# Diagonal products of a PEER layer as 64x64 tiles of the PE array

## The chip, the cores and the metric

The kernel runs as one program on one core of a Trainium2 chip. The metric is device time in microseconds (us) from start to end of the program. Before the change it is 4265.8 us, the median of three runs (4264.91 to 4271.66).

## The reference, cut to what matters

One layer of a diffusion backbone is applied to 128 context tokens and 1024 latent tokens of width 1024, all in float32. A token mixer comes first (two recurrences and a gated merge), then PEER: for every token, 8 heads choose 16 experts each out of 16384, and each chosen expert is one row `u` and one row `v` of a table.

```
def block(args):                      # hb: tokens x 1024, eb, gb: tokens x 8 heads x 16
    act = gelu(einsum('td,thkd->thk', hb, u_tab[eb]))
    return einsum('thk,thkd->td', gb * act, v_tab[eb])
...
out   = PEER(rmsnorm(x) * (1 + sc2) + sh2)
y     = rmsnorm(x + g2 * out, norm_f)
```

So a token has 128 chosen experts, and its output is the sum over them of `coefficient * v row`. Every row is gathered by an index that depends on the data. `u` and `v` of one expert lie side by side in memory (2048 floats, 8 KB).

## The kernel before, in words

The program has two parts. The first (to about 1275 us of the trace) is the mixer and its merge; the change touches it nowhere. The second is PEER. It handles the 1152 tokens as 9 tiles of 128 tokens, one token per partition. A tile has 128 chosen experts per token, one "slot" each: 4 pairs of heads x 32 slots. The slots are processed in rounds of 8 (`RING = 8`), because there are 8 ring buffers `RG[:, s, :]` of 128 x 2048 floats (1 MB).

One slot passes through five engines:

- **GpSimd queue** (`stage_b_pool`, `fetch`): waits until `v_used` says that the last user of this ring buffer is done (line 414), then issues one indirect DMA (line 415) that gathers 128 rows of 8 KB, one per partition.
- **VectorE** (`stage_b_dve`, `rounds`): when the rows have landed, a multiply with sum (line 845) gives the dot product with `u`. After every second slot (`GRP = 2`) `coef` (line 835) multiplies GELU by gate.
- **ScalarE** (`stage_b_act`, `rounds`): GELU (line 630), then for each slot a diagonal matrix (line 636): the identity times the slot's coefficient per partition, 128 x 128, into `DG[:, s, :]`, and counts `diag_r` up.
- **TensorE** (`stage_b_pe`, `rounds`): multiplies that diagonal matrix by the `v` half of the ring buffer, in two products of 512 columns (line 541), which accumulate in PSUM banks 0 and 1. All 128 slots of a tile accumulate there. Then it counts `v_used` up, which lets GpSimd refill the buffer.

The order of each engine's work is written out by hand. Between slots, at positions given by dictionaries called `between`, TensorE also does the queries, transposes and scores of the next tile (lines 482, 490, 498, 504), in banks 2 to 6; ScalarE copies them out, and VectorE searches the best keys. While tile 0 runs, this next-tile work is packed more tightly (`two_pairs_between`).

At the end of a tile VectorE copies the expert numbers and the next tile's input to where they are used (`next_tile`, lines 864 to 866), and the loop over tiles goes round. VectorE then does slots 0 and 1 of the new tile, and after slot 1 `read_sum` (line 877): it waits for all `v_used` of the old tile, reads banks 0 and 1, multiplies by the gate row `G2B` into `Y`, and counts `acc_free` up. TensorE waits for that, clears the two banks with products of a zero matrix (`clear`, line 550; two products), and only then goes on with the diagonal products of the new tile. After slot 5 `residual` (lines 883, 884) adds the residual and sums squares; after slot 11 `norm` makes the output. There are 8 such tile changes: from tile 0 into the loop over tiles 1 to 7, six from turn to turn of that loop, and one out of it to tile 8. After the last tile `read_sum`, `residual` and `norm` stand at the very end.

## Time and profile before

| what | value |
|---|---|
| median of three runs | 4265.8 us |
| the profiled execution's own time | 4269.28 us |
| its span, from first to last instruction | 4267.2 us |
| PE busy | 3688.6 us (86%) |
| VectorE busy | 2605.5 us (61%) |
| ScalarE busy | 1080.1 us (25%) |
| GpSimd busy | 1307.4 us (31%) |
| mean granted TensorE clock | 0.971 of full speed |

"Busy" is the time in which an engine has at least one instruction under way. PE's matmuls and PE's weight loads (PEld) are listed apart and overlap. Times of single instructions come from this one profiled execution. The granted clock is 1.0 at 2.4 GHz and 0.5 at 1.2 GHz; a figure between is a mean over a stretch.

### The profile page before, as it was taken

Reading aid. Unit: us, or ns where it says so; the run is one execution under the profiler, and the core shown is the slowest. Engines: PE = TensorE matmul, PEld = TensorE weight load, DVE = VectorE, ACT = ScalarE, POOL = GpSimd, SP = SyncE. Lnnn points to the kernel's source line nnn. Section 1 sums busy time; section 2 is a strip of 40 time slices with the busy share of each in tenths; the row PEclk is TensorE's granted clock in tenths of the full one; section 3 lists DMA queues with packets and bytes.
Section 4 is the critical chain, followed back from the end, with each engine's and each line's share of the span. In section 5 each row is a group of like instructions: output and inputs, shape, how many; then the busy total and the mean of one; then the engine's idle time right before and its main releaser. Section 6 shows DMA issues by size and latency. Waiting matters only on the chain.

```text
span 4267.2 us, 40396 instructions
## 1 busy us (share of the span) xinstructions
PE 3688.6 (86%) x10642; PEld 1802.4 (42%) x10642; DVE 2605.5 (61%) x6424; ACT 1080.1 (25%) x2672; POOL 1307.4 (31%) x1174
## 2 busy tenths in 40 slices
PE   8999999999997888888898888888888888888776
PEld 3766767555443333333333333333333333333222
DVE  4545455333238677667767766766776677677555
ACT  2534534000002223222222222222222222222211
POOL 0000000000003434444444444444444444444432
PEclk9999999999998999999999999999999999999999
DMA  4010000311429999999999999999999999999998
GB/s 175 16 35 20 25 10 32 129 69 69 182 73 361 420 400 407 420 420 401 413 419 400 420 422 399 421 419 393 421 421 389 420 422 400 417 417 420 413 422 356
DMA packets 187700, 1310.84 MB, mean 307 GB/s; under 512 B 24082, under 2 KB 25618, under 8 KB 36274
## 3 DMA queue, kind: packets, MB, share of 16 engines
q0 software_dynamic: 165888, 1208.03, 68.6%
q1 hardware_dynamic: 21684, 101.33, 6.2%
q8 instruction: 52, 0.85, 0.1%
q14 instruction: 76, 0.62, 0.1%
HBM read 1299.28 MB, written 10.00 MB: 307 GB/s over the span
## 4 chain that ended last, share of the span: by engine, by line
PE 47%; DMA 32%; DVE 9%; issue 9%; ACT 3%; DVEq 0%; POOL 0%; POOLq 0%; SPq 0%; ACTq 0%
DMA arena<-in_uv,arena 32%; PE ps L541 16%; PE ps L1101 9%; PE ps L449 9%; DVE arena L845 3%; PE ps L490 3%; PE ps L473 3%; PE ps L1145 2%; PE ps L1095 2%; ACT arena L636 1%; PE ps L1162 1%; PE ps L1117 1%; DVE arena L791 1%; PE ps L504 0%; DVE arena L795 0%
## 5 line engine op out<-in xcount | busy, mean ns | idle before, releaser
L541 PE MATMUL ps<-arena 128*128 128x512 f32 x4608 | 2201.6, 619 | 471.0 <-ACT arena L636 469.3
L845 DVE CUSTOM_DVE_ANT_0 arena<-arena 128x1024 f32<-128x1024 f32 x1152 | 1409.5, 1226 | 892.5 <-DMA arena<-in_uv,arena 831.4
L415 POOL DMA_INDIRECT arena<-in_uv,arena x1152 | 1301.2, 1130 | 1688.5 <-PE ps L541 1536.2
L541 PEld LDWEIGHTS ps<-arena 128*128 128x128 f32 x4608 | 864.1, 196 | 1723.1 <-issue 885.0
L636 ACT ACTIVATE arena<-ident,arena 128x128 f32<-128x128 f32 x1152 | 398.6, 393 | 1063.1 <-DVE arena L835 1063.1
L1101 PE MATMUL ps<-arena 128*128 128x384 f32 x1152 | 387.8, 493 | 15.9 <-issue 14.0
L406 POOL IOTA arena<- 128x16 f32 x1 | 0.1, 147 | 1244.6 <-DMA x_scratch<-arena 1244.6
L449 PE MATMUL ps<-arena 128*128 128x384 f32 x1152 | 373.9, 487 | 2.2 <-DMA arena<-in_w_mg 2.0
L630 ACT ACTIVATE arena<-arena 128x2 f32<-128x2 f32 x576 | 117.1, 203 | 1001.5 <-DVE arena L845 1001.4
L1101 PEld LDWEIGHTS ps<-arena 128*128 128x128 f32 x1152 | 217.8, 193 | 160.6 <-issue 22.8
L449 PEld LDWEIGHTS ps<-arena 128*128 128x128 f32 x1152 | 218.1, 190 | 159.7 <-issue 6.0
L490 PE MATMUL ps<-arena 128*128 (+1 forms) x576 | 284.1, 592 | 1.3 <-ACT arena L596 1.3
L1486 DVE SCALAR_TENSOR_TENSOR arena<-arena,dec,ps 128x128 f32<-128x128 f32 x272 | 94.6, 348 | 125.4 <-PE ps L1145 118.0
L490 PEld LDWEIGHTS ps<-arena 128*128 128x128 f32 x576 | 109.3, 190 | 138.7 <-issue 138.7
L697 DVE TENSOR_TENSOR arena<-ps,arena 128x384 f32<-128x384 f32 x48 | 24.5, 552 | 231.2 <-ACT arena L583 231.2
L473 PE MATMUL ps<-arena 128*128 128x512 f32 x288 | 123.8, 592 | 1.6 <-DVE arena L701 1.6
L583 ACT ACTIVATE arena<-ps 128x384 f32<-128x384 f32 x48 | 20.9, 488 | 362.4 <-PE ps L449 362.4
L1210 ACT ACTIVATE arena<-ps 128x384 f32<-128x384 f32 (+2 forms) x88 | 45.1, 517 | 245.9 <-PE ps L1101 201.5
L1264 ACT ACTIVATE arena<-ps 32x128 f32<-32x128 f32 x288 | 77.3, 268 | 85.9 <-PE ps L1135 82.8
L835 DVE TENSOR_TENSOR arena<-arena 128x2 f32<-128x2 f32 x576 | 90.3, 157 | 8.9 <-ACT arena L630 8.9
L845 DVE DVE_READ_ACCUMULATOR2_ANT arena<- 128x1 f32 x1152 | 94.5, 82 | 0.0
L1145 PEld LDWEIGHTS ps<-arena 128*128 128x128 f32 x576 | 74.9, 192 | 23.6 <-ACT arena L1264 11.5
(200 smaller groups left out, 2438.8 us busy)
## 6 DMA issues: line engine op xcount, KB each, us to landing
arena<-in_w_mod SPq DMA_DIRECT2D x12, 2048.0 KB, 23.3
arena<-in_uv,arena POOLq DMA_INDIRECT x1152, 10.3
arena<-in_w_in SPq DMA_DIRECT2D x28, 512.0 KB, 3.4
arena<-in_w_mg SPq DMA_DIRECT2D x8, 1536.0 KB, 6.2
arena<-x_scratch SPq DMA_DIRECT2D x18, 512.0 KB, 11.7
arena<-in_w_q SPq DMA_DIRECT2D x4, 2048.0 KB, 20.2
arena<-in_xT SPq DMA_DIRECT2D x4, 1152.0 KB, 13.4
arena<-in_x_tok SPq DMA_DIRECT2D x9, 512.0 KB, 4.7
```

The costliest lines, as they stand in the source:

```text
L415: nc.gpsimd.indirect_dma_start(out=RG[:, s, :], out_offset=None, in_=uv, in_offset=bass.IndirectOffsetOnAxis(ap=IDXS[:, par_, s:s + 1], ax ...
L449: mm = nc.tensor.matmul(PS[:, b + g, 0:CH], WMG[u][:, w0 + k, :], src[:, k, sl], start=(k == 0), stop=(k == nk - 1))
L473: mm = nc.tensor.matmul(PS[:, 2 * (t % 2) + n, :], MG[:, k, t * P:(t + 1) * P], WO[:, k, n * 512:(n + 1) * 512], start=(k == 0), stop=(k = ...
L490: mm = nc.tensor.matmul(PS[:, 4, :], H2T[:, k, :], WQ[:, k, bass.ds(i * 512, 512)], start=(k == 0), stop=(k == KD - 1))
L541: mm = nc.tensor.matmul(PS[:, n, :], DG[:, s, :], RG[:, s, D + n * 512:D + (n + 1) * 512], start=False, stop=False, skip_group_check=True)
L630: A(GEL[:, sl], PRE[:, sl], ACT.Gelu_apprx_tanh).then_inc(gel_r, 1)
L636: A(DG[:, s, :], ident[:], ACT.Copy, scale=COEF[:, s:s + 1]).then_inc(diag_r, 1)
L835: v.tensor_tensor(COEF[:, sl], GEL[:, sl], GATE[:, bass.ds(i * RPP * RING + q * RING + g * GRP, GRP)], ALU.mult).then_inc(coef_r, 1)
L845: ins = v.tensor_tensor_reduce(RG[:, s, 0:D], RG[:, s, 0:D], H2C, 1.0, 0.0, ALU.mult, ALU.add, PRE[:, s:s + 1])
L1101: mm = nc.tensor.matmul(z, w[:, k, :], hT[:, k, n * CH:(n + 1) * CH], start=(k == 0), stop=(k == KD - 1))
L1145: mm = nc.tensor.matmul(PS[:, 5 + it % 2, j * P:(j + 1) * P], KET[:, it % 2, j, :], Vt[:, tile_of(it), :], start=True, stop=True)
L1486: ins = v.scalar_tensor_tensor(out=to, in0=st, scalar=dec[:, d, c:c + 1], in1=PS[:, 5 + it % 2, j * P:(j + 1) * P], op0=ALU.mult, op1=ALU.add)
```

## The change: what it does

For each pair of slots TensorE waits once, for both diagonals. A diagonal matrix has nothing outside its two diagonal 64 x 64 blocks. So each slot's diagonal is now stored as 128 x 64: rows 0 to 63 hold the first block, rows 64 to 127 the second (`halves` is the identity in that form, made once by ScalarE into the tile `ones`, which is no longer used by then). Each product of 128 x 128 by 512 columns becomes two products of 64 x 64 by 512 columns, one per half of the partitions. The even slot of a pair writes them straight, and the odd slot swapped: rows 0 to 63 go to output partitions 64 to 127 and the other way round. So the four products of a pair with the same columns use four different quarters of the array. The two halves of the rows have accumulators of their own, banks 0 and 1 for rows 0 to 63, banks 2 and 3 for rows 64 to 127, and in each of them one half of the partitions holds the straight sum and the other the swapped sum.

What follows from that: `clear` zeroes four banks; the transposes of the input of the next tile (`front`) move from banks 2 and 3 to banks 4 and 7; `read_sum` copies the swapped halves into `Y` and adds the straight halves (four instructions on 64 partitions each, with a wait after each copy), and the multiplication by `G2B` moves to `residual`.

```
 def rounds(t, i, between):                         # TensorE
     for q in range(RPP):
-        for s in range(RING):
-            n0 = (t * ROUNDS + i * RPP + q) * RING + s + 1
-            pe.wait_ge(diag_r, n0)
+        for g in range(RING // GRP):
+            n0 = (t * ROUNDS + i * RPP + q) * RING + (g + 1) * GRP
+            wait_alone(pe, diag_r, n0)
             for n in range(2):
-                mm = nc.tensor.matmul(PS[:, n, :], DG[:, s, :], RG[:, s, D + n * 512:D + (n + 1) * 512],
-                                      start=False, stop=False, skip_group_check=True)
-            mm.then_inc(v_used, 1)
-            at = q * RING + s
-            if at in between:
-                between[at]()
+                for turned in range(GRP):
+                    s = g * GRP + turned
+                    for r in range(2):
+                        rows = slice(r * HALF, (r + 1) * HALF)
+                        c = (r + turned) % 2
+                        mm = nc.tensor.matmul(PS[c * HALF:(c + 1) * HALF, 2 * r + n, :], DG[rows, s, :],
+                                              RG[rows, s, D + n * 512:D + (n + 1) * 512],
+                                              start=False, stop=False, skip_group_check=True)
+            mm.then_inc(v_used, GRP)
+            for at in range(q * RING + g * GRP, q * RING + (g + 1) * GRP):
+                if at in between:
+                    between[at]()
 def clear():
-    for n in range(2):
+    for n in range(4):
         nc.tensor.matmul(PS[:, n, :], zero[:], zero[:, 0:1].to_broadcast([P, 512]), ...)
 def front(tn):
-    mm = nc.tensor.transpose(PS[:, 2 + k // 4, ...], H2N[...], ident[:])
+    mm = nc.tensor.transpose(PS[:, 4 + 3 * (k // 4), ...], H2N[...], ident[:])
 def stage_b_act(act):                              # ScalarE
+    for r in range(2):
+        rows = slice(r * HALF, (r + 1) * HALF)
+        A(halves[rows], ident[rows, rows], ACT.Copy).then_inc(hv_r, 1)
...
-    A(DG[:, s, :], ident[:], ACT.Copy, scale=COEF[:, s:s + 1]).then_inc(diag_r, 1)
+    A(DG[:, s, :], halves, ACT.Copy, scale=COEF[:, s:s + 1]).then_inc(diag_r, 1)
 def read_sum(self):                                # VectorE
     dve.wait_ge(v_used, (t + 1) * ROUNDS * RING)
-    v.tensor_tensor(Y, PS[:, 0:2, :]..., G2B, ALU.mult).then_inc(acc_free, 1)
+    halves_of = [slice(r * HALF, (r + 1) * HALF) for r in range(2)]
+    acc = [PS[:, 2 * r:2 * r + 2, :]... for r in range(2)]
+    for r in range(2):
+        self.ch(v.tensor_copy(Y[halves_of[r]], acc[r][halves_of[1 - r]]))
+    for r in range(2):
+        ins = v.tensor_tensor(Y[halves_of[r]], acc[r][halves_of[r]], Y[halves_of[r]], ALU.add)
+    ins.then_inc(acc_free, 1)
 def residual(self):
+    self.ch(v.tensor_tensor(Y, Y, G2B, ALU.mult))
     self.ch(v.tensor_tensor(Y, Y, XE, ALU.add))
```

## Rows read from the trace of the kernel before

**Rows 1.** The page: busy time of PE, transfer rate in 40 slices, the gather's queue.
```profile
PE 3688.6 (86%) x10642; PEld 1802.4 (42%) x10642; DVE 2605.5 (61%) x6424; ACT 1080.1 (25%) x2672; POOL 1307.4 (31%) x1174
GB/s 175 16 35 20 25 10 32 129 69 69 182 73 361 420 400 407 420 420 401 413 419 400 420 422 399 421 419 393 421 421 389 420 422 400 417 417 420 413 422 356
q0 software_dynamic: 165888, 1208.03, 68.6%
```
**Rows 2.** Stretches: busy time and count per engine, PEclk, DMA share, GB/s.
```profile
2240.00:2260.00 20.00, 17.34 (x42) 7.44 (x41) 15.87 (x56) 4.19 (x13) 10.26 (x9) 0.91 1.01 422
2300.00:2320.00 20.00, 19.55 (x52) 8.64 (x51) 14.07 (x28) 7.42 (x17) 9.78 (x9) 1.00 0.80 313
...
4220.00:4240.00 20.00, 14.92 (x33) 5.75 (x32) 10.29 (x21) 3.59 (x12) 7.62 (x9) 1.00 1.01 421
```
**Rows 3.** The same in stretches of 10 us, start of the gathering and end of tile 0.
```profile
1290.00:1300.00 10.00, 1.81 (x2) 0.84 (x3) 9.79 (x23) 1.91 (x5) 0.00 (x0) 0.50 1.02 428
1310.00:1320.00 10.00, 10.00 (x27) 4.53 (x26) 2.68 (x8) 1.27 (x4) 2.80 (x3) 1.00 0.94 350
...
1580.00:1590.00 10.00, 10.00 (x25) 4.39 (x24) 9.54 (x35) 2.17 (x7) 3.10 (x4) 1.00 0.98 361
```
**Rows 4.** The page's groups of instructions: diagonal products, queries.
```profile
L541 PE MATMUL ps<-arena 128*128 128x512 f32 x4608 | 2201.6, 619 | 471.0 <-ACT arena L636 469.3
L490 PE MATMUL ps<-arena 128*128 (+1 forms) x576 | 284.1, 592 | 1.3 <-ACT arena L596 1.3
```
**Rows 5.** Timeline, weight loads and a run of matmuls of line 541 (start, duration).
```profile
2400.42 1.88 PE L541 MATMUL ps<-arena 128*128 128x512 f32 x4
2400.43 0.19 PEld L541 LDWEIGHTS ps<-arena 128*128 128x128 f32 x1 [0.24 <-issue]
...
2400.85 0.19 PEld L541 LDWEIGHTS ps<-arena 128*128 128x128 f32 x1 [0.24 <-issue]
...
2401.28 0.19 PEld L541 LDWEIGHTS ps<-arena 128*128 128x128 f32 x1 [0.24 <-issue]
```
**Rows 6.** Waits from 1500 to 4260 us: who for whom, us, times, longest.
```profile
PE ps L550 <- DVE arena L877: 42.1, 8, 7.0
```
**Rows 7.** Timeline of one tile change inside the tile loop.
```profile
2610.64 7.28 PE L541 MATMUL ps<-arena 128*128 128x512 f32 x16 [1.73 <-ACT arena L636]
...
2620.84 1.23 DVE L845 CUSTOM_DVE_ANT_0 arena<-arena 128x1024 f32<-128x1024 f32 x1 [5.79 <-issue]
...
2623.13 1.22 DVE L877 TENSOR_TENSOR arena<-ps,arena 128x1024 f32<-128x1024 f32 x1
...
2624.41 3.49 PE L550 MATMUL ps<-zero 128*128 128x512 f32 x4 [6.49 <-DVE arena L877]
...
2627.73 7.25 PE L541 MATMUL ps<-arena 128*128 128x512 f32 x16
...
2630.39 1.14 POOL L415 DMA_INDIRECT arena<-in_uv,arena  x1 [10.76 <-PE ps L541]
```
**Rows 8.** Timeline of another such tile change, clear and first products.
```profile
3283.52 3.78 PE L550 MATMUL ps<-zero 128*128 128x512 f32 x4 [6.51 <-DVE arena L877]
3287.10 10.03 PE L541 MATMUL ps<-arena 128*128 128x512 f32 x20
3291.03 1.95 POOL L415 DMA_INDIRECT arena<-in_uv,arena  x1 [12.31 <-PE ps L541]
```
**Rows 9.** VectorE's groups by form: copies and two-input operations.
```profile
L866 DVE COPY arena<-arena 128x1024 f32<-128x1024 f32 x8 | 5.6, 698 | 0.0
L1465 DVE COPY arena<-ps 128x128 f32<-128x128 f32 x36 | 10.2, 283 | 0.0
L1467 DVE TENSOR_TENSOR arena<-ps,arena 128x128 f32<-128x128 f32 x36 | 10.2, 284 | 11.9 <-PE ps L1162 11.9
```
**Rows 10.** Timeline of the last tile change.
```profile
3936.51 0.94 POOL L415 DMA_INDIRECT arena<-in_uv,arena  x1 [0.30 <-issue]
...
3936.96 1.99 PE L550 MATMUL ps<-zero 128*128 128x512 f32 x4 [1.31 <-DVE arena L877]
...
3941.04 1.22 DVE L845 CUSTOM_DVE_ANT_0 arena<-arena 128x1024 f32<-128x1024 f32 x1 [1.26 <-DMA arena<-in_uv,arena]
```
**Rows 11.** Timeline of the program's end.
```profile
4251.39 7.13 PE L541 MATMUL ps<-arena 128*128 128x512 f32 x16 [1.27 <-ACT arena L636]
...
4258.56 1.22 DVE L877 TENSOR_TENSOR arena<-ps,arena 128x1024 f32<-128x1024 f32 x1 [4.85 <-PE ps L541]
4259.82 1.23 DVE L883 TENSOR_TENSOR arena<-arena 128x1024 f32<-128x1024 f32 x1
```

More of the change, by code:

```diff
@@ L56 @@
 GRP = 2
+HALF = P // 2
 P_LB, P_CW, P_CB, P_BR, P_BI, P_LAM, P_HN, P_H0, NPAR = 0, 4, 8, 9, 11, 13, 15, 16, 18
@@ L274, in build @@
     QS, QTS = QQ[:, 0:512], QQ[:, 512:1024]
-    DG = DG_.rearrange("p (s c) -> p s c", s=RING)
+    DG = DG_[:, 0:RING * HALF].rearrange("p (s c) -> p s c", s=RING)
     SCS, SCW = SC_[:, 0:512], SC_[:, 512:1024]
@@ L299, in build @@
     PRE, GEL, COEF = sm(RING), sm(RING), sm(RING)
+    halves = ones[:, 0:HALF]
     PHL = sb("places", [P, 2, 2, TOPK], U32)[:]
@@ L314, in build @@
     acc_free, e_sq, e_sd, y_r, y_st = (sem(x) for x in ("acc_free", "end_square", "end_sd", "y_ready", "y_stored"))
-    it_r = sem("iota_ready")
-    PAIR_STEPS, FRONT_STEPS, END_STEPS = 16, 2, 2
+    it_r, hv_r = sem("iota_ready"), sem("half_identities_ready")
+    PAIR_STEPS, FRONT_STEPS, END_STEPS = 16, 2, 5
     def row(ap):
@@ L481, in front @@
             for k in range(KD):
-                mm = nc.tensor.transpose(PS[:, 2 + k // 4, (k % 4) * P:(k % 4 + 1) * P],
+                mm = nc.tensor.transpose(PS[:, 4 + 3 * (k // 4), (k % 4) * P:(k % 4 + 1) * P],
                                          H2N[:, k * P:(k + 1) * P], ident[:])
@@ L595, in rows_out @@
             for n in range(2):
-                cp = A(H2T_[:, n * 512:(n + 1) * 512], PS[:, 2 + n, :], ACT.Copy)
+                cp = A(H2T_[:, n * 512:(n + 1) * 512], PS[:, 4 + 3 * n, :], ACT.Copy)
             cp.then_inc(h2t_e, 1)
@@ L652, in stage_b_act @@
         rows_out(0)
+        act.wait_ge(hv_r, 2)
         for i in range(2):
@@ L876, in read_sum @@
                 dve.wait_ge(v_used, (t + 1) * ROUNDS * RING)
-                v.tensor_tensor(Y, PS[:, 0:2, :].rearrange("p b c -> p (b c)"), G2B, ALU.mult).then_inc(acc_free, 1)
+                halves_of = [slice(r * HALF, (r + 1) * HALF) for r in range(2)]
+                acc = [PS[:, 2 * r:2 * r + 2, :].rearrange("p b c -> p (b c)") for r in range(2)]
+                for r in range(2):
[3 more added lines that the diff above has]
+                ins.then_inc(acc_free, 1)
             def residual(self):
```

## The prediction

> **What bounds the kernel now.** I read the page first, then stretches of equal length, then the timeline at the places where the stretches differ. The page invites a wrong reading: PE is busy 86% of the span [rows 1], and its costliest group is the one that is changed, 2201.6 us [rows 4]. But the transfer rate in the same page stands at 420 to 422 GB/s in most slices from the fourteenth on and falls only in every third or so. The stretches say what that is: in the middle of a tile the DMA share is 1.01 at 422 GB/s, while PE is busy 17.34 of 20 us; in the last tile, where PE has nothing but diagonal products, PE is busy only 14.92 of 20 and the rate is the same, 421 [rows 2]. The rate doesn't follow PE. So the gathering is bound by its transfers: a slot is 1 MB, at 422 GB/s 2.48 us, and 1152 slots are 1208 MB, 2860 us of the span. PE needs 1.71 us for a slot (below) and waits 471 us for diagonals, that is for data [rows 4].
>
> The transfers lose time in two kinds of places only. Adding up, in stretches of 10 us from 1280 to 4250, what is missing to 422 GB/s gives 76 us. Some 19 us of it lie in tile 0 where PE is busy 10.00 of 10 us and the rate is 350 to 361 [rows 3], at its start and its end (VectorE too is at 9.54 in the second). Some 34 us lie at the six tile changes inside the tile loop, 4 to 7 us each: in 2300 to 2320 the share is 0.80 at 313 GB/s [rows 2]. There PE stops at 2617.92 with all the old tile's slots done, VectorE comes out of the loop's turn only at 2620.84 (5.79 us of "issue"), does two slots, and reads the sum at 2623.13; PE clears, and the first ring buffer comes free so late that the next gather is issued at 2630.39, after 10.76 us without one [rows 7]. The ring of eight is empty by then. The first and last tile change have no such pause: PE waits 42.1 us at all eight [rows 6], which is about 6.6 at the six and 1.3 at each of the other two.
>
> So a faster PE can win back only the 19 us, and what lengthens the way from VectorE's read to the first free buffer is paid in full, six times.
>
> **The change part by part.** All sums are made against the profiled execution (4269.28 us, span 4267.2) and carried as differences to the median, 4265.8, which lies 3.5 below it.
>
> *The diagonal products.* A product of 512 columns is issued as two couples of weight load and matmul: 4608 matmuls for 2304 products [rows 4]. The loads start 0.42 to 0.43 us apart [rows 5], so a matmul takes 0.427 us, a slot four of them, 1.71 us, a pair 3.42. After the change a pair has eight products and so sixteen couples. No product of the trace uses a part of the array, so the price of a pair must be bounded. Above: nothing overlaps, 16 x 0.427 = 6.83 us. Below: four quarters run at once, 1.71 us. Between them stands the order of issue. The two couples of one product use the same quarter, and the second can't stream before the first has; if matmuls start in program order, the next product's first couple can only start beside the second couple of this one. Then each product adds one matmul's time: eight of them, 8 x 0.427 = 3.42 us a pair, just what it was. I take that value: it is the only one of the three for which the code gives a reason, since couples of one product stand next to each other and nothing in the change interleaves products. The Trainium skill (TensorE: Matmul & The Clock Gate, "Part 3: Packing small matmuls — row/col tiling") says both that matmuls of different tiles overlap with some 4 ns between starts, and that matmuls keep strict program order; the first alone would give 1.71 us a pair, both together 3.42 by my count of couples. No run here shows either.
>
> In the middle of tiles none of these but the uppermost shows, because transfers hide it: a pair of slots brings 4.97 us of transfer, PE has some (284.1 us of queries + 29 of clears) / 576 = 0.54 us of other work per pair [rows 4], so PE may take up to 4.4 us a pair. The one wait per pair releases the even slot's buffer 1.71 us later; PE is followed by four gathers in flight, so nothing there. ScalarE's diagonals get shorter and stay hidden beside the same transfers.
>
> *read_sum.* Before: one instruction, 1.22 us [rows 7]. After: two copies out of PSUM and two additions, 1024 elements wide each. No row shows that fewer partitions cost less, so 64 are priced like 128. A copy of 128 columns out of PSUM costs 283 ns and a two-input operation 284 [rows 9], so I price a copy of 1024 like the 1.22 us operation (the SBUF copy's 0.698 us [rows 9] is the lower end). With a wait behind each copy the four start about 1.26, 1.26 and 1.15 us apart: 4.87 us, 3.65 more than before (2.6 with the cheap copies). `acc_free` comes that much later. Queued behind it on VectorE are slots 2 and 3; their diagonals move by as much, and PE's restart moves further, so they don't come last. The 1.25 us added to `residual` stand behind slot 5, where at least six buffers are already being used up: they lie beside the refilling. The transposes that move to banks 4 and 7 wait for the same copies as before and cost nothing.
>
> *clear.* Two more products, four more matmuls: 1.71 us at full clock, 3.4 at half. PE has idled some 6.5 us before; the clear takes 3.49 and 3.78 us for four matmuls, which is half clock [rows 7, 8]. In rows 7 the products after it are already at full clock (16 in 7.25 us); in rows 8 the first ones aren't, since the first gather comes 7.5 us after the clear's start instead of 6.0. Since the time at half clock is spent anyway, the added matmuls fall largely behind the rise and cost 1.71 us.
>
> *First release.* The old kernel frees one buffer after four matmuls, the new one two after eight: 1.71 us later where a pair takes 3.42, nothing where it takes 1.71.
>
> Per tile change in the loop: 3.65 + 1.71 + 1.71 = 7.1 us, and the transfers already stand still there, so six of them are 42.5 us. (Bounds: 2.6 + 1.7 + 0 = 4.3 us, 26 in all; 3.65 + 3.4 + 3.4 = 10.5, 63 in all.) At the other two tile changes the last gather is issued at 3936.51 and slots land to about 3951 (slot 3 is waited for at 3941.04 [rows 10], four more follow at 2.48 us); a restart 7 us later frees two buffers at about 3947.6: hidden, I put 2 us for both. The Trainium skill (TensorEngine Tiling (Array Packing), "Key Properties") adds that a change of tiling mode drains the engine, which each step between the pairs would now bring twice; the trace has no such change and transfers hide it but in tile 0's packed stretches. For those and the lone wait per pair, and for the later first release at the start (PE at half clock, up to 3.4 us), I put 4 us, between 0 and 10.
>
> *The end.* Both last pairs' diagonals are there long before PE is through (16 matmuls, 7.13 us), then everything is in series [rows 11]: 3.65 us of read_sum and 1.25 for the multiplication that moves to `residual` (4259.82 to the next start). 4.9 us.
>
> Sum: 42.5 + 2 + 4 + 4.9 = 53 us. 4265.8 + 53 = 4319 us.
>
> **The rivals.**
>
> *All four quarters run at once* (1.71 us a pair). For it: nothing in a row forbids it. Then PE's stretches in tile 0 go (1.71 us for a slot and 1.71 for the two queries behind it become 0.85 and 1.71), of 19 us some 10, VectorE holding the rest; the end gains 2.2 us because the last pair takes 1.8 us instead of two slots' 3.4 and more. Per change 3.65 + 1.71 = 5.4, six times 32; 32 - 10 + 4.9 - 2.2 = 25: 4291 us. So the change's aim reached in full is still slower.
>
> *Faster than before.* Quarters at once, and the buffers that come free sooner keep more gathers in flight. With eight queued and PE idle the rate was 428 GB/s, against 422 with some four in flight [rows 2, 3]. Over 2860 us that is 1.4%, 40 us: 4291 - 40 = 4251 us. It decides from a rate of about 426 on. Against it: 422 holds in the last tile as in the busiest stretches, and 428 is one stretch of 10 us.
>
> *Weight loads show.* If the load of the next product can't run while a matmul waits, each of the eight products brings up to a load's 0.19 us [rows 5]: 8 x 0.62 = 4.9 us a pair, with the other work 5.5, over the 4.97 of transfer: PE bound, 576 x 0.5 = 290 us and some of the above, about 4590 us. With half the load, for half the columns, it just stays hidden, 4340.
>
> *Nothing overlaps*, so the change doesn't do what it says: 6.83 + 0.54 = 7.37 us a pair, 576 x 2.4 = 1380 us, 5650 us. For it: no row shows two matmuls at once.
>
> **How the numbers follow.** A pair as long as before 0.45 (4319; its own range 4298 to 4345 from the bounds above); four at once 0.22 (4291, down to 4275); faster by deeper queueing 0.08 (4251); loads show 0.11 (4340 to 4590); no overlap 0.14 (5650). What a measurement of this kernel tells from no change is about 0.2%, 8.5 us. Faster 0.07, within it 0.06 (cheap copies with four at once, or a part of the higher rate), slower 0.87. The range leaves out the last case and the upper part of the one before: 4250 to 4440.
>
> **What would show it.** In the profile after: the rate in mid-tile still 422 with a share of 1.01; at the six tile changes a DMA gap of 11 to 13 us instead of 4 to 7; between VectorE's first copy of `read_sum` and `acc_free` 4.9 us; eight matmuls in the clear; PE's busy time for a pair 3.4 us (or 1.7, or 6.8); the chain of waits at the end 4.9 us longer. Wrong would make it: a mid-tile rate off 422 in either direction, PE busy near 20 of 20 us in mid-tile, or a first gather after the tile change not later than before.

## The result, and the profile after

The changed kernel takes 4318.6 us (median of four runs, 4316.15 to 4320.49); the kernel before, in four runs, takes 4268.5 (4264.91 to 4271.66). The ratio is 1.0119, with a 95% interval of 1.0103 to 1.0135: 50 us slower. The profiled execution took 4319.78 us, its span is 4317.9, 50.7 more than the span before.

The page of the changed kernel, lines that answer to those of before [rows 1, 4]: busy times, granted clock and transfer rate in 40 slices, the costliest group.

```profile
PE 3118.9 (72%) x15286; PEld 1363.4 (32%) x15286; DVE 2648.6 (61%) x6460; ACT 1018.3 (24%) x2674; POOL 1286.5 (30%) x1174
PEclk9999999999997887887887887788878887878777
GB/s 173 16 34 20 25 10 43 115 68 73 183 108 372 413 404 379 414 421 377 413 422 380 418 422 377 417 422 376 415 417 377 415 412 384 419 418 409 415 420 346
L548 PE MATMUL ps<-arena 64*64 64x512 f32 x9216 | 1495.2, 778 | 1047.5 <-ACT arena L647 1046.9
```

The diagonal products have twice as many matmuls (9216 for 4608) and a third less busy time (1495 us for 2202): TensorE does gain. The rate still reaches 420 to 422 in the good slices; the dips, 389 to 401 before, are 376 to 384 now. The granted clock, 0.971 on the mean before, is 0.863, and 7 to 8 tenths in every slice of the gathering, where PE now idles between pairs.

Stretches of the changed kernel, in columns as before: mid-tile, one tile change, last tile, and three stretches of tile 0 [rows 2, 3].

```profile
2240.00:2260.00 20.00, 13.37 (x78) 4.28 (x76) 10.24 (x21) 4.35 (x14) 7.53 (x8) 0.95 1.01 422
2640.00:2660.00 20.00, 9.54 (x40) 3.42 (x40) 17.75 (x24) 5.69 (x12) 2.02 (x3) 0.66 0.56 223
4220.00:4240.00 20.00, 11.35 (x68) 2.98 (x64) 10.48 (x22) 3.16 (x12) 8.96 (x9) 0.74 1.01 422
...
1310.00:1320.00 10.00, 8.75 (x44) 2.86 (x42) 3.73 (x8) 1.16 (x4) 4.16 (x4) 1.00 1.00 401
1580.00:1590.00 10.00, 8.25 (x36) 2.96 (x40) 9.43 (x37) 1.97 (x6) 5.13 (x5) 1.00 1.01 420
1610.00:1620.00 10.00, 5.28 (x32) 1.49 (x32) 9.33 (x35) 1.38 (x5) 5.83 (x4) 0.83 0.86 318
```

In mid-tile and in the last tile the rate is what it was, 422 at a share of 1.01. The tile change is where it differs: 0.56 and 223 GB/s. In tile 0 PE is no longer busy 10.00 of 10 us and the rate rises there (401 for 350, 420 for 361); thirty microseconds later VectorE is busy 9.33 of 10 and the rate is 318. In the kernel before VectorE was as busy in that stretch (9.33) and the rate was 371, so its share alone doesn't say why. Adding up what is missing to 422 GB/s, as the prediction did, gives 24.0 us from 1290 to 1640 before and 23.5 in the changed kernel: what PE gave back early in that packed stretch is lost late in it. Over the whole gathering the same sum is 76 us before, 122 in the changed kernel.

The timeline of a tile change of the changed kernel (start, duration, instruction, idle time before it) [rows 7].

```profile
2642.00 1.23 DVE L857 CUSTOM_DVE_ANT_0 arena<-arena 128x1024 f32<-128x1024 f32 x1 [5.97 <-issue]
...
2644.29 2.47 DVE L892 COPY arena<-ps 64x1024 f32<-64x1024 f32 x2
...
2646.80 2.46 DVE L894 TENSOR_TENSOR arena<-ps,arena 64x1024 f32<-64x1024 f32 x2
...
2649.31 5.95 PE L558 MATMUL ps<-zero 128*128 128x512 f32 x8 [12.02 <-DVE arena L894]
...
2655.19 3.66 PE L548 MATMUL ps<-arena 64*64 64x512 f32 x32
...
2657.95 0.94 POOL L417 DMA_INDIRECT arena<-in_uv,arena  x1 [17.68 <-PE ps L548]
```

The same two dot products and 5.97 us of loop turn stand ahead. Then the read takes 4.97 us (2644.29 to 2649.26) where one instruction took 1.22; the clear takes 5.88 (to 2655.19) where it took 3.32; and the first pair already runs at full clock. From the first touch of the sum to the next gather it is 13.66 us; before, 7.26. GpSimd is without a released buffer for 17.68 us, before for 10.76.

To say how much of that is lost for good, a marker is needed that doesn't depend on how many gathers are queued. I take the mean start of VectorE's dot products of slots 56 to 71 of each tile, worked out from the trace's records: in the middle of a tile these follow the landing of the rows. Time between markers of neighbouring tiles is then the price of a tile and its change. Differences to the profiled execution of before, in us, good to about 0.1:

| kernel | start to tile 0 | change 0 to 1 | six changes in the loop | change 7 to 8 | end | span |
|---|---|---|---|---|---|---|
| before (us itself) | 1459.9 | 334.5 | 1976.0 | 323.4 | 173.2 | 4267.2 |
| changed | +3.2 | +6.7 | +35.0 | +2.7 | +3.3 | +50.7 |
| full-array products, new boundary | +2.9 | +9.1 | +32.3 | +2.8 | +4.8 | +51.8 |
| new read_sum alone | +2.0 | +5.9 | +26.1 | +1.5 | +4.8 | +40.1 |
| four banks cleared alone | +1.1 | +3.5 | +6.9 | -1.2 | 0.0 | +10.2 |
| changed, straight quarters | +21.7 | +29.0 | +159.0 | +22.9 | +7.8 | +240.3 |
| before, grouped in pairs | +17.3 | +20.9 | +112.6 | +13.8 | +0.3 | +164.7 |
| changed, two quarters per slot | +8.3 | +8.4 | +42.4 | +4.4 | +4.7 | +68.1 |
| changed, no clear | -0.7 | +4.1 | +37.1 | +2.0 | +3.1 | +45.6 |
| changed, ScalarE reads | +2.9 | +6.7 | +20.0 | +4.2 | +3.7 | +37.3 |

Of the first column most is scatter of the mixer, where no kernel differs: the first dot product starts anywhere from 1293.7 to 1300.9 in these executions (1294.1 before, 1297.6 in the changed kernel). Of the 50.7 us, 44.4 are tile changes, 35.0 of them the six in the loop.

Each row is one execution. `e11` below, which differs from the changed kernel in the order of its products alone, has +31.1 in the column of the six changes, and `e7` and `e8`, whose times are within 0.1% of before, have +1.7 and -0.5 there. So differences of 4 us in that column, 0.6 a change, say nothing.

### The profile page after: what moved, and what is told of

It is laid out like the page before. It is cut to its first block, busy times and chain, and to the rows that moved or that the text cites. A ratio compares the mean times of both kernels' runs of the same rounds, so it can differ in the third digit from the quotient of the medians.

```text
span 4317.9 us, 49824 instructions
## 1 busy us (share of the span) xinstructions
PE 3118.9 (72%) x15286; PEld 1363.4 (32%) x15286; DVE 2648.6 (61%) x6460; ACT 1018.3 (24%) x2674; POOL 1286.5 (30%) x1174
## 4 chain that ended last, share of the span: by engine, by line
PE 41%; DMA 31%; issue 12%; DVE 12%; ACT 3%; POOL 1%; DVEq 0%; POOLq 0%; SPq 0%; ACTq 0%
DMA arena<-in_uv,arena 30%; PE ps L548 12%; PE ps L1120 9%; PE ps L451 9%; DVE arena L857 4%; PE ps L475 3%; PE ps L1164 2%; ACT arena L647 2%; PE ps L1114 1%; PE ps L1181 1%; POOL arena L417 1%; PE ps L492 1%; DVE arena L745 1%; PE ps L1136 1%; DVE arena L744 1%
## 5 line engine op out<-in xcount | busy, mean ns | idle before, releaser
L548 PE MATMUL ps<-arena 64*64 64x512 f32 x9216 | 1495.2, 778 | 1047.5 <-ACT arena L647 1046.9
L417 POOL DMA_INDIRECT arena<-in_uv,arena x1152 | 1280.3, 1111 | 1752.9 <-PE ps L548 1499.1
L548 PEld LDWEIGHTS ps<-arena 64*64 64x64 f32 x9216 | 410.9, 162 | 2039.4 <-issue 2039.2
L647 ACT ACTIVATE arena<-ones,arena 128x64 f32<-128x64 f32 x1152 | 337.0, 340 | 1066.2 <-DVE arena L847 1059.2
L492 PE MATMUL ps<-arena 128*128 (+1 forms) x576 | 297.1, 638 | 1.3 <-ACT arena L607 1.3
L1120 PEld LDWEIGHTS ps<-arena 128*128 128x128 f32 x1152 | 218.6, 193 | 159.9 <-issue 23.4
L451 PEld LDWEIGHTS ps<-arena 128*128 128x128 f32 x1152 | 218.1, 190 | 159.7 <-issue 6.0
L492 PEld LDWEIGHTS ps<-arena 128*128 128x128 f32 x576 | 100.3, 195 | 203.2 <-issue 203.2
L475 PE MATMUL ps<-arena 128*128 128x512 f32 x288 | 123.8, 592 | 1.6 <-DVE arena L713 1.6
L558 PE MATMUL ps<-zero 128*128 128x512 f32 x72 | 52.3, 892 | 82.2 <-DVE arena L894 82.2
L594 ACT ACTIVATE arena<-ps 128x384 f32<-128x384 f32 x48 | 20.9, 488 | 362.0 <-PE ps L451 362.0
## 6 DMA issues: line engine op xcount, KB each, us to landing
arena<-in_w_mod SPq DMA_DIRECT2D x12, 2048.0 KB, 23.5
arena<-in_xT SPq DMA_DIRECT2D x4, 1152.0 KB, 13.8
```

Of the source, the lines that this page charges most:

```text
L417: nc.gpsimd.indirect_dma_start(out=RG[:, s, :], out_offset=None, in_=uv, in_offset=bass.IndirectOffsetOnAxis(ap=IDXS[:, par_, s:s + 1], ax ...
L451: mm = nc.tensor.matmul(PS[:, b + g, 0:CH], WMG[u][:, w0 + k, :], src[:, k, sl], start=(k == 0), stop=(k == nk - 1))
L475: mm = nc.tensor.matmul(PS[:, 2 * (t % 2) + n, :], MG[:, k, t * P:(t + 1) * P], WO[:, k, n * 512:(n + 1) * 512], start=(k == 0), stop=(k = ...
L492: mm = nc.tensor.matmul(PS[:, 4, :], H2T[:, k, :], WQ[:, k, bass.ds(i * 512, 512)], start=(k == 0), stop=(k == KD - 1))
L548: mm = nc.tensor.matmul(PS[c * HALF:(c + 1) * HALF, 2 * r + n, :], DG[rows, s, :], RG[rows, s, D + n * 512:D + (n + 1) * 512], start=False ...
L647: A(DG[:, s, :], halves, ACT.Copy, scale=COEF[:, s:s + 1]).then_inc(diag_r, 1)
```

## The experiments

Times are medians; each ratio is to the kernel before, run on the same chip. `e11` alone has a single run.

### The boundary with the old products

`e1`: before's diagonal products, everything else of the tile change and of the end as in the changed kernel.

```
 # before, plus:
-END_STEPS = 2
+END_STEPS = 5
 clear():      -for n in range(2)      +for n in range(4)
 front():      -PS[:, 2 + k // 4, ...] +PS[:, 4 + 3 * (k // 4), ...]
 read_sum():   -Y = PS[0:2] * G2B      +two copies and two additions on 64 partitions
 residual():                           +Y = Y * G2B
```

> The kernel before, its full-array products and one wait per slot kept, with the whole tile change of the changed kernel: four banks cleared, four instructions to read the sum, the gate multiplication in residual. PE's products cost what they did, 3.42 us a pair. Theory T1 (all the added time is read_sum, clear and the longer end, whatever the products cost): per tile change 3.7 us of reading and 2.5 us of clearing, six times 6.2, some 9 us at the other two, 4.9 us at the end: 4267 + 51 = 4318, like the changed kernel. Theory T2 (a good part comes from the emptier, colder PE of the changed kernel, granted clock 0.81 in mid-tile): the boundary alone gives about half, 4290.

Measured: 4317.5 us, ratio 1.0117 (1.0101 to 1.0132), clock 0.966. With products as long as they were and one release per slot, the time is that of the changed kernel. The timeline of its tile change shows the same chain:

```profile
2648.22 2.48 DVE L880 COPY arena<-ps 64x1024 f32<-64x1024 f32 x2
...
2650.73 2.46 DVE L882 TENSOR_TENSOR arena<-ps,arena 64x1024 f32<-64x1024 f32 x2
...
2653.24 5.47 PE L550 MATMUL ps<-zero 128*128 128x512 f32 x8 [10.31 <-DVE arena L882]
...
2661.20 1.43 POOL L415 DMA_INDIRECT arena<-in_uv,arena  x1 [16.56 <-PE ps L541]
```

Two things follow. The tile change and the end account for the whole difference; added up as above, 121 us are missing to 422 GB/s here, 122 in the changed kernel. And the lower clock costs nothing that the total shows: 0.966 here, 0.863 in the changed kernel, same time.

### read_sum alone, the clear alone

`e2` has only the new `read_sum` and `residual` (both halves from banks 0 and 1, with a maximum for the sum); `e3` has only the four-bank clear and the moved transposes.

```
 e2: read_sum(): +copy PS[0:2] to Y, half by half; +Y = max(PS[0:2], Y), half by half
     residual(): +Y = Y * G2B
 e3: clear():    -for n in range(2)       +for n in range(4)
     front():    -PS[:, 2 + k // 4, ...]  +PS[:, 4 + 3 * (k // 4), ...]
```

> The kernel before with only the reading changed: read_sum in four instructions of 64 partitions, the gate multiplication in residual; two banks cleared as before. T1: six times 3.7 and some 4 at the other two, 4.9 at the end: 31 us more, 4298. T2: the same 4.9 at the end, and half of the rest, 4285.

> The kernel before with only four banks cleared instead of two (and the transposes of the next tile in banks 4 and 7). T1: 1.7 to 2.5 us at each of six tile changes, little at the other two: 10 to 18 us more, about 4281. T2 says the same of this run, since the clear falls into half clock either way; nothing at all would mean that VectorE's chain to the first diagonal is late instead.

Measured: `e2` 4308.8 us, ratio 1.0093 (1.0077 to 1.0108); `e3` 4279.2, ratio 1.0031 (1.0020 to 1.0042). Over the kernel before on their chip (4267.7) that is 41.1 + 11.5 = 53 us together, and `e1`, which has both, is 49.8 over it: the whole, within the scatter. `e2` came out 11 us above what I had expected; the table says where: the two changes outside the loop cost 5.9 and 1.5, and a change in the loop 26.1 / 6 = 4.4, where the read is 3.75 us longer. The clear costs 6.9 / 6 = 1.2 per change in the loop.

### Are four quarters at work, and do they matter?

`e4`: the odd slot is written straight too, so a pair has two quarters only.

```
-                        c = (r + turned) % 2
+                        c = r
```

> The changed kernel with the odd slot written straight like the even one: only two of the four quarters of the array are used, nothing else is changed (the swapped halves stay zero). If quarters run side by side, a pair takes 8 x 0.43 = 3.4 us at full clock instead of 1.73, as long as in the kernel before, and PE is busier and warmer. T1: the time hardly moves, 4318 to 4322 (the last pairs at the end add up to 2 us, the first pair of each tile 1.7 us times six: at most 4330). T2: a warmer PE gives back some of what the cold one costs: 4305 or less.

Measured: 4512.0 us, ratio 1.0574 (1.0560 to 1.0589). Both theories were wrong, and by 180 us. The timeline of the changed kernel, PE and its weight loads:

```profile
2401.19 3.64 PE L548 MATMUL ps<-arena 64*64 64x512 f32 x16 [4.33 <-ACT arena L647]
...
2406.13 0.24 PEld L548 LDWEIGHTS ps<-arena 64*64 64x64 f32 x8 [1.07 <-issue]
2406.16 1.95 PE L548 MATMUL ps<-arena 64*64 64x512 f32 x16 [0.27 <-ACT arena L647]
2406.61 0.18 PEld L548 LDWEIGHTS ps<-arena 64*64 64x64 f32 x4 [0.25 <-issue]
2407.04 0.18 PEld L548 LDWEIGHTS ps<-arena 64*64 64x64 f32 x4 [0.25 <-issue]
```

and of the kernel with straight quarters:

```profile
2576.92 3.65 PE L548 MATMUL ps<-arena 64*64 64x512 f32 x16
2580.50 1.98 PE L492 MATMUL ps<-arena 128*128 x4
2582.41 3.65 PE L548 MATMUL ps<-arena 64*64 64x512 f32 x16
```

In the changed kernel the 16 matmuls of a pair go in four beats of four, 0.43 us apart (loads of the first two beats together at 2406.13, then at 2406.61 and 2407.04), and the pair is through in 1.95 us, tail included. That is all four quarters at once. Pairs that follow each other directly start 1.77 us apart. A pair that comes after 4.33 us of idle PE runs at half the clock and takes 3.64. With straight quarters there are eight beats, 3.65 us at full clock (3.43 from start to start), and where queries stand between the pairs the period is 5.49 us (2576.92, 2582.41). The transfer of a pair takes 4.97. So pairs of 3.4 us, which my prediction called hidden, aren't hidden in this kernel. Whether that is their length or something else in the change is the next question.

### Is it the length of the pair, or the grouping?

`e5` is the kernel before with one wait and one release per pair of slots, which also moves the next tile's work from behind each slot to behind the pair; nothing else changes. `e12` is `e4` (every slot written straight) with a wait and a release per slot, and the next tile's work back behind each slot. Below, "grouping" means these three together: wait, release, and place of the other work.

```
 e5:  -for s in range(RING): pe.wait_ge(diag_r, n0); two products; mm.then_inc(v_used, 1); between[at]()
      +for g in range(RING // GRP): wait_alone(pe, diag_r, n0); four products
      +    mm.then_inc(v_used, GRP); between[...] of both slots
 e12: -for g in range(RING // GRP): ... mm.then_inc(v_used, GRP)
      +for s in range(RING): wait for slot s; PS[rows, 2 * r + n, :] for r, n; mm.then_inc(v_used, 1)
```

> The kernel before with its full-array products, its boundary, and only the grouping of the changed kernel: one lone wait for both diagonals of a pair, one release of both buffers after both, the next tile's work behind the pair. The two-quarter run was 190 us slower than the changed kernel although its pair takes 3.5 us, no more than two slots of the kernel before. Theory G (the grouping costs, and four quarters at once pay for it): with 3.42 us a pair this run is slower than the kernel before by 100 us or more, since PE is occupied 3.4 + 1.7 us where two queries follow, more than the 4.97 of transfer, and the first buffer of each pair comes free late. Theory D (it is the change between 64x64 and 128x128 products that costs in the two-quarter run, some 0.1 to 0.2 us each way): this run has no such change and stays within 20 us of the kernel before.

> The changed kernel with two quarters per slot (straight only) and a wait and a release for each slot, as in the kernel before; boundary as changed. Two slots take 3.4 us at full clock, as in e4, and the change between 64x64 and 128x128 products happens twice as often. Theory G (grouping two slots is what made e4 and e5 slow): back to the boundary-only run, 4318 to 4335. Theory D (the change of shape drains the array): as slow as e4 or slower, 4450 to 4550.

Measured: `e5` 4441.6 us, ratio 1.0414 (1.0399 to 1.0430); `e12` 4338.9, ratio 1.0168 (1.0153 to 1.0184). Theory G is borne out in both, though `e12` ends 4 us above its range. Grouping alone costs before's kernel 173 us; taking it away from straight quarters gives back 173 of the 193 us that these had cost. In `e5`, PE, ScalarE and GpSimd in a stretch with next-tile work:

```profile
2475.20 3.67 PE L542 MATMUL ps<-arena 128*128 128x512 f32 x8 [1.36 <-ACT arena L637]
...
2479.34 0.60 ACT L606 ACTIVATE arena<-ps 128x512 f32<-128x512 f32 x1 [4.20 <-PE ps L498]
...
2479.84 0.68 ACT L637 ACTIVATE arena<-ident,arena 128x128 f32<-128x128 f32 x2
...
2480.66 3.67 PE L542 MATMUL ps<-arena 128*128 128x512 f32 x8 [1.36 <-ACT arena L637]
...
2479.65 1.42 POOL L415 DMA_INDIRECT arena<-in_uv,arena  x1 [2.90 <-PE ps L542]
2481.37 0.94 POOL L415 DMA_INDIRECT arena<-in_uv,arena  x1 [0.30 <-issue]
2485.12 0.94 POOL L415 DMA_INDIRECT arena<-in_uv,arena  x1 [2.81 <-PE ps L542]
```

PE waits 1.36 us for diagonals ahead of each pair, and the pairs come 5.46 us apart instead of 4.97. In these rows it is a circle between PE and ScalarE that sets the 5.46: the transposes of the next tile (line 498) stand behind the pair of 2475.20, ScalarE waits 4.20 us for them, copies them out at 2479.34, makes the next two diagonals only then, at 2479.84, and PE's next pair waits for these. From 1720 to 3960 us ScalarE waits 296 us in all for queries, transposes and scores in `e5`, 92 in the kernel before.

A second reading is that of the buffers. Two are freed together, at the end of the second slot's products; their gathers go out together, and then none for 3 to 4 us. The first slot's buffer is held longer, by its wait for the second slot's diagonal and by the second slot's products (1.7 us), and eight buffers are all there are: at 2.48 us a slot, the way from gather to gather may take 19.8 us. Which of the two makes how much of the loss isn't shown: no run takes the wait, the release and the place of the other work apart (and ScalarE's waits alone prove little, since `e12` has 254 us of them and loses only 20 us to the changed kernel). The 173 us are measured. Stretches of `e5`, 100 us mid-tile and in the last tile, then 10 us each inside the first:

```profile
2560.00:2660.00 100.00, 81.12 (x184) 34.93 (x183) 60.31 (x163) 21.07 (x61) 43.17 (x37) 0.91 0.97 379
4300.00:4400.00 100.00, 73.71 (x162) 28.83 (x160) 51.80 (x105) 17.94 (x60) 51.50 (x40) 1.00 1.01 422
...
2580.00:2590.00 10.00, 8.99 (x20) 3.49 (x18) 7.29 (x21) 1.10 (x4) 5.11 (x5) 0.96 0.91 310
2630.00:2640.00 10.00, 10.00 (x24) 4.29 (x23) 5.22 (x12) 1.79 (x6) 5.46 (x4) 1.00 1.01 424
```

In the last tile, where no engine has work for a next tile, the rate is 422 even so; mid-tile it is 379. Inside the mid-tile stretch it isn't low where queries stand between PE's pairs (2630: 424, PE busy 10.00 of 10) but after them, where PE has pairs alone and VectorE searches keys (2580: 310). I read that so: the dense stretch uses up what the ring has in hand, and the rate falls only behind it. The changed kernel shows no such loss: its total is that of `e1`, which isn't grouped, and its mid-tile rate is 422. I put that down to its pair, which takes 1.77 us, about the 1.72 that one slot took.

In `e12` the slots with one query each come 2.92 us apart; in `e1`, 2.58. Both have four beats of 0.43 for the slot and two for the query, so going from 64 x 64 to the full array and back costs 0.34 us. The starts of single matmuls show it spread: 0.10 us ahead of the query, 0.10 between the query's own two matmuls, 0.09 ahead of the next slot and 0.05 in its first beat. It isn't the lone wait per slot, since slots of `e12` without a query between them start 1.72 us apart, as before:

```profile
2583.26 1.94 PE L545 MATMUL ps<-arena 64*64 64x512 f32 x8
2585.12 1.13 PE L492 MATMUL ps<-arena 128*128 x2
2586.18 1.93 PE L545 MATMUL ps<-arena 64*64 64x512 f32 x8
```

### The order of the products

`e11`: the changed kernel with the two products of one quarter next to each other, all of slot 0's upper half first, and so on.

```
-for n in range(2):
-    for turned in range(GRP):
-        for r in range(2):
+for turned in range(GRP):
+    for r in range(2):
+        for n in range(2):
```

> The changed kernel with the loops turned: both products of one quarter follow each other, then the next quarter. My prediction held that couples of one quarter next to each other keep the array from running more than two quarters at once; in the changed kernel four matmuls start within 0.02 us of each other every 0.43 us although each product is two couples. If TensorE looks past a matmul that waits for its quarter, this order costs the same, 1.75 us a pair, 4318. If it starts in program order and the couples of the four products are interleaved when the program is built, this order brings two matmuls of a quarter in a row and the pair takes longer, 2.6 to 3.4 us, and the time goes to 4400 or more.

Measured, a single run: 4313.8 us, about that of the changed kernel (4316.2 to 4320.5). Its timeline:

```profile
2403.65 0.26 PEld L548 LDWEIGHTS ps<-arena 64*64 64x64 f32 x8 [1.31 <-issue]
...
2403.68 1.97 PE L548 MATMUL ps<-arena 64*64 64x512 f32 x16 [0.51 <-ACT arena L647]
...
2404.13 0.21 PEld L548 LDWEIGHTS ps<-arena 64*64 64x64 f32 x4 [0.22 <-issue]
```

(The records don't name the quarter; this takes it that the matmuls reach TensorE in the order of the code.) Of the two orders tried, neither is slower.

### The tile change without its clear

`e6` and `e7` take the clear out of the changed kernel and of the kernel before: the first product of a tile overwrites its bank instead.

```
-start=False, ...
+start=(first products of a tile), ...
-clear()
```

> The changed kernel without the clears: the first pair of a tile starts its accumulation instead (start on the eight products of the first pair). T1 (the tile change is on the path): the clear took 5.9 us between acc_free and the first pair, but the first pair then runs at half clock (3.6 instead of 1.8 us), so about 4 us are saved per change, six times 4 and some at the other two: 4318 - 28 = 4290. If instead VectorE's chain to the diagonals 0 and 1 is next (they are there 1.3 us after acc_free), only a little less is saved, 4295.

> The kernel before without its clears in the same manner. The clear took 3.3 to 3.5 us between acc_free (2624.35 in the trace before) and the first product (2627.73); the diagonals are there at 2626.7. So 1 to 2 us are saved per change at most, and the first slot then runs at half clock, 1.7 us more: T1 expects nothing to 10 us in all, 4258 to 4268.

Measured: `e6` 4314.4 us, ratio 1.0104 (1.0089 to 1.0120); `e7` 4269.6, ratio 1.0003 (0.9994 to 1.0012). In `e7` taking the old clear out gains nothing, as expected. `e6` was expected at 4290 and gains 4. Its tile change:

```profile
2645.94 3.69 PE L548 MATMUL ps<-arena 64*64 64x512 f32 x16 [14.09 <-ACT arena L646]
...
2650.43 1.71 POOL L417 DMA_INDIRECT arena<-in_uv,arena  x1 [15.61 <-PE ps L548]
...
2650.96 3.69 PE L548 MATMUL ps<-arena 64*64 64x512 f32 x16 [1.33 <-ACT arena L646]
...
2656.99 1.95 PE L548 MATMUL ps<-arena 64*64 64x512 f32 x16 [2.34 <-ACT arena L646]
```

Without the clear the first two pairs run at half clock, and they wait for diagonals, since VectorE, which has spent 5 us on the sum, owes PE the slots behind it: 9.82 of 10 us busy from 2640. The next gather comes 15.61 us after the last free buffer instead of 17.68; none of this reaches the markers (+37.1 over six changes, +35.0 with the clear). So read_sum costs twice, through `acc_free` and through VectorE's own queue. Taking 5.9 us of clear away gains 4 us in eight changes, because what it frees is taken up by the second wait and by the pairs at half clock; this run doesn't separate the two.

### Can the reading leave VectorE?

ScalarE reads the sum instead: in `e8` right after the last diagonals, ahead of the row norm; in `e9` with the row norm moved behind the first slot; in `e10` the same as `e9` in the changed kernel (four copies on 64 partitions, one addition left to `residual`).

```
 ScalarE: +wait v_used; A(Y, PS[0:2], ACT.Copy).then_inc(acc_free, 1)     (e8, e9)
          +wait v_used; four copies of halves to Y and OH_               (e10)
          -0: row_norm(tn)   +0.5: row_norm(tn)                          (e9, e10)
 VectorE: -read_sum()        residual(): +Y = Y * G2B  (e10: +Y = Y + OH_ first)
```

> The kernel before, with ScalarE reading the sum out of PSUM as soon as the last product is in (it idles 8.8 us there), and the gate multiplication in VectorE's residual. acc_free comes at about 2619.3 instead of 2624.35, the clear runs at full clock beside VectorE's two dot products, and PE then waits for the diagonals 0 and 1, which come 1.15 us earlier, too, since VectorE has no read_sum before slot 2. T1: first gather about 2.5 to 4 us earlier per change, six times, less 1.2 us at the end: 4267 - 18 = 4249. If the tile change isn't what bounds, no change.

> The kernel before with ScalarE reading the sum (as e8) and the next tile's row norm on ScalarE moved behind the first two diagonals of a tile. In e8 acc_free and the clear were early, but ScalarE's square, table load and square root (2626.71 to 2629.4) stood between the first GELU and the first diagonal, and the first gather came no earlier. Theory: the first gather of a tile change is set by whichever of acc_free plus clear and the first diagonal is last; with both early it comes 1.6 to 3.5 us sooner, six times: 4273 - 15 = 4258, some 10 us under the kernel before. If VectorE's front then waits for the row norm and holds slot 4, part of it is lost again, 4268.

> The changed kernel with ScalarE reading both sums of both halves (four copies, while it idles 9.2 us) before VectorE comes out of the loop's turn, and the row norm behind the first diagonals. acc_free comes before VectorE's first slot instead of 4.9 us after its second; the clear runs beside the two dot products. Theory T1: the tile changes fall back to what they cost in the kernel before, 36 + 9 us less; the end has three more instructions of 1.25 us and four copies in series, 4 us more than now: 4318 - 41 = 4277. With the row norm out of the way another 10 less, 4267. If the products as quarters cost something by themselves in mid-tile, it stays above 4290.

Measured: `e8` 4273.1, ratio 1.0011 (1.0002 to 1.0020); `e9` 4281.1, ratio 1.0028 (1.0018 to 1.0038); `e10` 4304.7, ratio 1.0085 (1.0071 to 1.0099). The first two were to be faster than before and are not. In `e8`:

```profile
2621.32 1.02 ACT L652 ACTIVATE arena<-ps 128x1024 f32<-128x1024 f32 x1 [3.50 <-PE ps L541]
2622.39 1.99 PE L550 MATMUL ps<-zero 128*128 128x512 f32 x4 [1.11 <-ACT arena L652]
...
2626.71 1.05 ACT L589 ACTIVATE arena<-arena 128x1024 f32<-128x1024 f32 x1
...
2629.37 0.68 ACT L636 ACTIVATE arena<-ident,arena 128x128 f32<-128x128 f32 x2
...
2634.37 1.03 POOL L415 DMA_INDIRECT arena<-in_uv,arena  x1 [11.37 <-PE ps L541]
```

the sum is read at once and the clear is done at 2624.4, but the row norm on the same engine stands before the first diagonals of the new tile, which start at 2629.37. In `e9` the row norm is out of that way, and now VectorE waits for it, with the later slots behind it:

```profile
2641.19 0.17 DVE L725 RECIPROCAL arena<-arena 128x1 f32<-128x1 f32 x1 [2.26 <-ACT arena L591]
...
2645.64 3.70 PE L541 MATMUL ps<-arena 128*128 128x512 f32 x8 [1.97 <-ACT arena L636]
```

`e10` is the one that helps, by a third of what was expected: 14 us less than the changed kernel instead of 41 or more. Its gaps without a released buffer in the loop are 9.0 to 10.4 us instead of 16.1 to 17.9, and the markers show 20.0 us over six changes instead of 35.0. It is still 36 us slower than before. Each time one wait was taken away, the next one stood close behind it.

## Why the prediction came out, and which of its steps failed

The time was predicted at 4319 and is 4318.6. That the tile changes and the end, and not the products, would decide it was right. That it fits to 1 us is luck: the four terms were forecast at 42.5, 2, 4 and 4.9 us, and the markers have 35.0, 9.4, 3.2 and 3.3, and the price of a pair, which stands behind the first of them, was wrong by a factor of two.

**Transfers bound the middle of a tile: right.** The rate is 422 at a share of 1.01 before and after, with PE busy 17.34 and 13.37 of 20 us, and even at a granted clock of 0.74 in the last tile.

**The step that failed: "each product adds one matmul's time ... 3.42 us a pair".** It rested on matmuls starting in program order, with a product's two couples on one quarter. They start in beats of four, a pair takes 1.77 us, and with couples of one quarter in a row (`e11`) it is the same. Rival "all four quarters at once", given 0.22, is what happens. The Trainium skill (TensorE: Matmul & The Clock Gate, "Part 3: Packing small matmuls — row/col tiling") says that matmuls of different tiles overlap, which this trace shows (the four starts of a pair's first beat lie within 0.02 us, those of its later beats within 0.05); and that their starts keep program order, which the 1.97 us of `e11` contradict, if the order of the code is the order of issue.

**"PE may take up to 4.4 us a pair" and "the one wait per pair ... nothing there": wrong.** `e5` has exactly that pair, 3.42 us with one wait and one release, and takes 4442. I had spread the queries evenly over all pairs (0.54 us each), where they stand in blocks, behind every slot of a stretch, and I had counted four gathers in flight without asking how long each buffer is away. So had PE behaved as I forecast, the time would have been about 4442 plus the boundary, some 4490 by my estimate (`e4`, whose pairs last that long, is at 4512): above my range. The mistake about the quarters hid the mistake about the grouping.

**Per tile change 7.1 us: near, 5.8 (35.0 / 6).** By terms:
- read_sum: +3.65 forecast. The four instructions take 4.97 us, 3.75 longer than 1.22, as forecast, each as dear as on 128 partitions. As a loss of time it is 4.4 per change (`e2`), some 0.5 more than the delay of `acc_free`, which is within the scatter; that slots 2 and 3 and the multiplication in `residual`, which stand behind it on VectorE, make the rest is my reading. "They don't come last" holds only while the clear stands there; `e6` shows that they do as soon as it is gone.
- clear: +1.71 forecast. It takes 5.88 us, 2.6 more, since the rise of the clock falls late in it; but the loss is 1.2 (`e3`); I take it that a part lies beside the late diagonals.
- first release: +1.71 forecast. The changed kernel less `e1` is 2.7 / 6 = 0.5, within the scatter of that column, so nothing is shown; a pair takes no longer than a slot did.

**The other two changes, 2 us for both: right for one.** The change 7 to 8, whose rows I had read [rows 10], costs 2.7. The change 0 to 1 costs 6.7, and I had priced it by the rows of the other. It follows tile 0's packed stretch, where VectorE is busy 9.3 of 10 us; that no buffers are ahead there is my reading, which no run tests.

**Tile 0 and the start, 4 us:** 3.2 to the marker of tile 0, but 3.5 of the first dot product's delay lie in the unchanged mixer. The 10 us that the rival expected PE to win back in tile 0 are not there, at most 2.4 (6.7 against 9.1 in `e1`, one execution each): the rate does rise where PE was the bound, and falls below that of before late in the stretch. That VectorE holds it there is likely, for the profile had it at 9.54 [rows 3], but no run shows it.

**The end, 4.9 us: 3.3.** With full-array products it is 4.8 (`e1`, `e2`). The quarters give 1.5 of it back, as the rival had it, though less than its 2.2:

```profile
4298.78 5.36 PE L548 MATMUL ps<-arena 64*64 64x512 f32 x32 [3.01 <-ACT arena L647]
4304.19 2.48 DVE L892 COPY arena<-ps 64x1024 f32<-64x1024 f32 x2 [3.38 <-PE ps L548]
...
4309.20 1.23 DVE L901 TENSOR_TENSOR arena<-arena 128x1024 f32<-128x1024 f32 x1
```

PE had been idle before its last two pairs and runs the first of them at half clock (granted clock 0.54 from 4298.8 to 4302.4), so 32 matmuls take 5.36 us and not the 3.66 of 2655.19. Here the low clock does cost its 1.7 us.

The rival that had the mechanism, all four quarters at once, had 25 us for the whole; the markers add to 50.9 (rounding included). The 26 us between are 16.7 in tile 0 and its change (it had -10, the markers have +6.7), 2.7 at the change 7 to 8, 2.6 in the six changes (35.0 against its 32.4), 0.6 at the end (3.3 against 2.7), and 3.2 in the first column, which is mostly the mixer's scatter.

**"Faster than before", by deeper queueing: not seen.** No rate above 422 appears in the changed kernel's slices, mid-tile or last tile, though buffers come free sooner.

## What to carry to other kernels

An engine that is 86% busy may still have nothing to give: ask in which stretches it, and not the transfers, sets the rate, and look at the other engines in just those stretches. A faster inner product was paid for with two more accumulators, and these are cleared and read in the one place where nothing hides it; weigh such work times the number of boundaries. In a ring that transfers fill, judge a grouping of waits and releases in the stretch in which other work is densest, by how long it holds a buffer and by what other engines wait for behind the group: the mean over all stretches said there was room, and 173 us were lost.

## What the runs showed of the hardware

- Four 64 x 64 float32 tiles of TensorE run side by side: 8 products of 64 x 64 by 512 columns in 1.77 us from start to start (1.95 with the tail), 3.43 (3.65) where only two quarters are used; two orders of issue gave the same.
- Going from 64 x 64 tiles to the full array and back cost 0.34 us (2.92 against 2.58 us for a slot and a query), spread over four starts. The Trainium skill (TensorEngine Tiling (Array Packing), "Key Properties") names the drain and gives no size for it.
- An addition of 64 partitions by 1024 out of PSUM takes VectorE 1.23 us (two in 2.46), as long as the multiplication of 128 by 1024 took (1.22); a copy of 64 by 1024 takes as long (two in 2.47).
- A pair after 4.33 us of idle PE ran at 1.2 GHz, 3.64 us (granted clock 0.53 from 2401.2 to 2404.8); the next, after a query and 0.27 us of idle, at 2.4 GHz, 1.95 us (1.00 from 2406.1 to 2408.1). The mean granted clock fell from 0.971 to 0.863; the total doesn't show it, and at the very end it cost 1.7 us.
